# A different spacing in SBUF of the activation buffers that TensorE reads, in a two-block network kernel

## The reference

```python
x = x + 0.5 * swiglu(rms_norm(x), w_gate, w_up, w_down)     # width 2816
x = x + hybrid_mixer(rms_norm(x), w_in, ...)                # dilated and stick-breaking attention
x = x + 0.5 * swiglu(rms_norm(x), w_gate2, w_up2, w_down2)
```

```python
x = x + rms_norm(mix(branches(h @ w_in), gates(h @ w_gate)) @ w_o)   # four branches
x = x + rms_norm((gelu(conv(gate)) * conv(val)) @ ffn_w_down)        # [gate, val] = h @ ffn_w_up
```

## Time and profile before

| what | us |
|---|---|
| median of 3 runs | 2228.83 |
| lowest and highest of the 3 | 2226.13, 2240.37 |
| the profiled execution, its own time | 2226.13 |
| span from its first to its last instruction | 2224.3 |
| mean granted clock of TensorE, as a share of full | 0.986 |

### The profile page before, as it was taken

One profiled execution on the slowest core, in us unless ns is written; L12 is line 12 of the kernel. 1 busy time (PEld: TensorE's weight loads), 2 busy tenths in 40 slices (PEclk: granted clock), 3 DMA queues, 4 the chain that ended last, 5 costly groups with the idle time before them and its releaser, 6 DMA issues.

```text
span 2224.3 us, 40846 instructions
## 1 busy us (share of the span) xinstructions
PE 2156.6 (97%) x17952; PEld 2079.5 (93%) x17952; DVE 1496.8 (67%) x1812; ACT 1100.4 (49%) x1334; POOL 126.4 (6%) x118
## 2 busy tenths in 40 slices
PE   8999999999999999999999799999999989999998
PEld 8999999999999999999999698989989879898998
DVE  5556757555655775755568996667766898666775
ACT  5435465444543446544442567555554365655553
POOL 0001000000100100000000000001000000000100
PEclk9999999999999999999999899999999989998999
DMA  7655535655555543555553444446554344353652
GB/s 257 203 178 170 167 126 169 202 189 176 186 190 187 169 157 133 171 191 189 187 183 116 136 153 136 134 144 209 192 177 134 118 148 151 117 175 111 208 190 76
DMA packets 285045, 367.26 MB, mean 165 GB/s; under 512 B 10003, under 2 KB 257731, under 8 KB 284611
## 3 DMA queue, kind: packets, MB, share of 16 engines
q1 hardware_dynamic: 281138, 361.01, 49.2%
q10 hardware_dynamic: 3728, 3.62, 0.5%
HBM read 363.56 MB, written 1.05 MB: 164 GB/s over the span
## 4 chain that ended last, share of the span: by engine, by line
PE 85%; DVE 9%; ACT 4%; issue 1%; DMA 1%; POOL 0%; ACTq 0%; SPq 0%; POOLq 0%; DVEq 0%
PE ps L619 25%; PE ps L620 24%; PE ps L621 24%; DVE wlo L1797 2%; ACT whi L1284 2%; PE ps L663 1%; PE ps L702 1%; PE ps L704 1%; PE ps L703 1%; DVE sq L2405 1%; PE ps L1051 1%; PE ps L1068 1%; PE ps L1078 1%; PE ps L1099 1%; DVE arena L2084 0%
## 5 line engine op out<-in xcount | busy, mean ns | idle before, releaser
L619 PE MATMUL ps<-hhi,whi 128*128 128x256 f32 x3808 | 1084.8, 285 | 17.0 <-DVE wlo L1797 6.6
L620 PE MATMUL ps<-hlo,whi 128*128 128x256 f32 x3808 | 1062.6, 279 | 0.0
L621 PE MATMUL ps<-hhi,wlo 128*128 128x256 f32 x3808 | 1062.5, 279 | 0.0
L1797 DVE TENSOR_TENSOR wlo<-raw,whi 128x2048 fp32r<-128x2048 f32 (+1 forms) x347 | 781.9, 2255 | 415.9 <-ACT whi L1284 415.7
L1284 ACT ACTIVATE whi<-raw 128x2048 fp32r<-128x2048 f32 (+1 forms) x347 | 653.0, 1885 | 701.5 <-PE ps L621 616.0
L619 PEld LDWEIGHTS ps<-hhi,whi 128*128 128x128 f32 x3808 | 719.9, 189 | 34.2 <-issue 13.3
L620 PEld LDWEIGHTS ps<-hlo,whi 128*128 128x128 f32 x3808 | 717.0, 188 | 4.8 <-issue 4.3
L621 PEld LDWEIGHTS ps<-hhi,wlo 128*128 128x128 f32 x3808 | 718.8, 189 | 0.2
L619 PE MATMUL ps<-hidhi,whi 128*128 128x256 f32 x1056 | 295.6, 280 | 1.9 <-DVE hidlo L2165 1.9
L621 PE MATMUL ps<-hidhi,wlo 128*128 128x256 f32 x1056 | 294.8, 279 | 0.0
L620 PE MATMUL ps<-hidlo,whi 128*128 128x256 f32 x1056 | 294.8, 279 | 0.0
(11 more groups left out here) (284 smaller groups left out, 2106.0 us busy)
## 6 DMA issues: line engine op xcount, KB each, us to landing
raw<-in_ffn_w_up SPq DMA_DIRECT2D x88, 1024.0 KB, 5.1
raw<-in_w_in SPq DMA_DIRECT2D x68, 1024.0 KB, 5.2
raw<-in_ffn_w_down SPq DMA_DIRECT2D x66, 1024.0 KB, 4.8
raw<-in_ffn_w_gate SPq DMA_DIRECT2D x43, 1024.0 KB, 5.1
raw<-in_w_gate SPq DMA_DIRECT2D x32, 1024.0 KB, 5.4
raw<-in_w_branch SPq DMA_DIRECT2D x16, 1024.0 KB, 4.9
raw<-in_nsa_cmp_w SPq DMA_DIRECT2D x8, 1024.0 KB, 5.4
raw<-in_w_out SPq DMA_DIRECT2D x6, 1024.0 KB, 4.8
```

The lines of the kernel that those rows point to most:

```text
L619: pe.matmul(o, w_hi, m_hi, start=start, stop=False, skip_group_check=True)
L620: pe.matmul(o, w_hi, m_lo, start=False, stop=False, skip_group_check=True)
L621: return pe.matmul(o, w_lo, m_hi, start=False, stop=stop, skip_group_check=True)
L1797: dve.tensor_tensor(wlo[:, slot, 0:n], raw[:, slot, 0:n], whi[:, slot, 0:n].bitcast(F32), ALU.subtract) \
```

## The change

The one spacer of 48 columns between `wlo` and `hhi` becomes six spacers of 16 columns, one before each of the six activation buffers. `arena` grows from 12624 to 12656 columns.

```diff
-ARENA = 12624
+ARENA = 12656
...
-        def phase(n, cols):
+        def phase(n):
-            return sb(f"phase{n}", cols)
+            return sb(f"phase{n}", 16)
-        phase(0, 48)
+        phase(0)
         hhi = view(sb("hhi", KC * SEQ, F32R), c=KC, t=SEQ)
+        phase(1)
         hlo = view(sb("hlo", KC * SEQ, F32R), c=KC, t=SEQ)
+        phase(2)
         hidhi = view(sb("hidhi", 2 * 2 * SEQ, F32R), b=2, c=2, t=SEQ)
+        phase(3)
         hidlo = view(sb("hidlo", 2 * 2 * SEQ, F32R), b=2, c=2, t=SEQ)
+        phase(4)
         brhi = view(sb("brhi", 2 * BRC * SEQ, F32R), b=2, c=BRC, t=SEQ)
+        phase(5)
         brlo = view(sb("brlo", 2 * BRC * SEQ, F32R), b=2, c=BRC, t=SEQ)
```

## The result

The changed kernel takes 2254.36 us (median of 6 runs, 2248.61 to 2258.47), the kernel before 2228.72 us (6 runs, 2210.04 to 2240.37). The ratio is 1.0115 with a 95% interval of 1.0077 to 1.0154: slower by about 1.15%. The profiled execution of the changed kernel took 2260.43 us, its span is 2258.6 us; before these were 2226.13 and 2224.3. That execution is not one of the six: it is the slowest of the nine on record for the changed kernel.

What follows compares the result with a forecast made beforehand. TensorE bounds the kernel: 15,552 full matmuls times their spacing, plus waits. No instruction changes, moved buffers and distance were each taken as 0, so 2226.1 us for the profiled execution, median 2229; range 2196 to 2266.

Steps and rivals of the forecast that it cites:

- the mixture stays: Full matmuls keep both spacings, 113.3 and 117.7 ns, in the same shares; median 2229 us, chance 0.42.
- the first rival: Matmuls on hhi, hlo and their followers all go to 117.7 ns; up to 35.5 us more, median 2264, chance 0.36.
- the wide spacing: In feed-forward windows at full clock, full matmuls starting 117.7 ns apart, 4.4 ns more than the other value.
- What bounds the kernel: TensorE, busy in 97% of the span: 15,552 full matmuls times their start-to-start spacing, plus some waits.
- The count and the step of the rival: 8079 full matmuls now at the smaller spacing, each 4.4 ns longer: 35.5 us more, 2261.6 us.
- close ones: Full matmuls starting about 113.3 ns apart; 8079 of them reckoned, against 7473 at 117.7 ns.
- The failed step: For the distance between weight slice and activation chunk, 0 us was taken: restarts pick the spacing and stay where they were.
- The hint for it: Token-major units, roles exchanged: all four windows hold 45 matmuls in 5 us, 117.7 ns; called not conclusive.
- The bound from above: All full matmuls at 120 ns, the highest spacing in any row, from 30-column ones: 71 us more, 2297.
- The bound on the other engines: Moved buffers of ScalarE, VectorE and GpSimd: 0 taken, 3 us either way if operations changed by 1%.
- The rule of separate read ports: TensorE reads moving operand and weights through separate ports and never waits, so placement costs nothing; sum stays 2226.1 us.
- The third rival: The two reads stop disturbing each other, weight loads set 111 ns per full matmul: 2157, median 2160 us, chance 0.05.

Runs made afterwards that it cites:

- the third set: Kernels with only hhi/hlo moved, only hidlo/brhi/brlo moved, or one spacer of 40 or 56 columns for 48; 2246.99, 2237.94, 2264.88, 2266.86 us against 2227.64.

## Why the prediction came out as it did

The point, 2229, and the likeliest case behind it, "the mixture stays" at 0.42, were wrong. The measured 2254 lies inside the range 2196 to 2266, but the range held it only because it reached to the first rival, the wide spacing becomes the rule, which had 0.36.

- *What bounds the kernel* was right. The loss is spacing of the full matmuls, nearly all of it: 37.4 us more busy time of TensorE, 3.1 us less waiting.
- *The count and the step of the rival* met the measurement, the step by luck. "8079 x 4.4 ns = 35.5 us more", 2261.6 for the profiled execution; it measured 2260.43, 34.3 us more. The median grew by 25.6 only, and 2264 for it was 10 us too high: the profiled execution of before lies 3 us below its median, the one after 6 us above its own. The count of 8079 close ones had a sampled third in it; the mean spacings of the trace (115.3, 116.1 and 115.8 ns, between 113.3 and 117.8) come to about 8000. The step of 4.4 ns was not to be had from the rows of before: 32 columns alone give 118.7 or 120 ns, and that 16 and 32 together come to the mean of the wide spacing, by another pattern, no row told.
- *The failed step* is "The value I take is 0, the same mixture of the two spacings, since rows 4 and 5 have both at one and the same distance: what picks one is how a stream restarts". Two spacings at one distance show that the distance alone does not fix the spacing. They do not show that it has no say. The experiments show that the distance (or the place, see the end of this section) sets which spacings are open to a stream (two at 48 and 32, one at 0, 56 and 64, nearly always one at 16, three at 40), and only then does something else pick among them.
- *The hint for it* was read but weighed too low. The token-major units, always wide, were "the one full-width case at another distance". With the pattern of 64 columns that the runs found, exchanged roles at 48 amount to a distance of -48, which is 16, and 16 gave 117.8 as well. That reading fits, but was not tried by itself. In the kernels with 16 and 80 columns, where exchanged roles amount to 48, three and four of the eight token-major units went to 113.4 ns; with 112, where they amount to 16, none did. That fits too.
- *The bound from above* of 120 ns met the value that all stretches have at 0 and 64 columns, but by rounding: by starts read to 1 ns no three of those 30-column matmuls take more than 119.3 ns each, and their mean is 116.2. It was priced at 2297 and measured 2281 and 2278. With no spacer the full-clock streams did grow by about 69 us, near the 71 of the sum; shorter pauses and less time at the lower clock (mean 0.988 against 0.986) gave part of it back.
- *The bound on the other engines*, 0 taken and 3 us allowed, held: with only their buffers moved the kernel stays in the scatter of before, though one run can't resolve 3 us.
- *The rule of separate read ports.* The Trainium skill, "SBUF — State Buffer", section "Who interferes with whom", by which the sum stays 2226, is not borne out by these runs: the same matmuls with the same loads are 113.4 to 120.0 ns apart, 6.6 ns each, by nothing but addresses.
- *The third rival*, a spacing below the close one, found nothing: 113.3 ns is the lowest in any long stretch of the 14 kernels.

Left open: what in the memory repeats every 64 columns (256 bytes), and what picks the close or the wide spacing at 48. That a restart picks it is seen in the earlier trace rows, in a stage that came out wide in one kernel and close in two others, and in the streams that never change without an interruption; what about the restart does it was not tried. Nor was a distance of `wlo` from `whi` other than whole weight slices. One rival is not separated by any edit: `raw`, `whi` and `wlo` stood still in all kernels, so each spacer changed the distance and the place of the activation buffers alike, and it could be the place that counts. The token-major units speak for the distance: there the weights move and the activations stand, and at 16, 48, 80 and 112 columns the spacings are those of the distance with its sign turned. A kernel with `whi` and `wlo` shifted and the activations left alone would decide it.

## What to carry to other kernels

In a stream of matmuls that each bring their own weight load, the spacing from start to start can hang on where the moving chunk stands against the weight slice in SBUF; here the same work took 2222 to 2281 us by the size of an empty spacer. Measure it by the count of matmuls in a busy window at full clock, not by whole runs, and treat the distance as a parameter to scan over one period. Here the scan found no point better than the one the kernel had. When one configuration shows two values for the same work, do not conclude that the configuration doesn't matter: ask whether another one takes the better value away.

## What the runs showed that was not expected

- The mean spacing takes few discrete values, and a stream keeps one for over a thousand matmuls: with all six buffers alike 113.4, 117.4, 117.8, 118.4, about 118.8 and 120.0 ns were seen, with 1, 2 or 3 of them open at a given distance. Below the mean lies a pattern that repeats: at 0 columns every distance is 120 ns, at 32 they go from 115 to 122.
- The pattern repeats at 64 columns, 256 bytes, half of a weight slice's length: 0 and 64, 16 and 80, 48 and 112 gave the same spacings.
- At 48 columns the runs of before scatter by 30 us (2210 to 2240); the changed kernel scatters by 12 (2249 to 2260, nine runs), and that goes with its mean granted clock to within about 2 us, from 0.990 down to 0.983. The clock does not explain the scatter at 48: in the third set the kernel before took 2223.33 us at 0.982 and 2239.6 at 0.981. That would fit stages of 1438 matmuls, 6.3 us each, that fall to one spacing or the other from run to run; it is not shown, since the spacings are known of profiled executions only.
- Giving the high and the low parts unlike distances, 48 and 64, was mostly worse (119.3 ns, in places 117.8) than 16 for both, but 16 and 32 for `hhi` and `hlo` was no worse than 16 for both (117.8 ns): the six distances can't be judged one at a time.
